# A channel mixer whose down projection multiplies paired halves of 512 columns, with the eight sample tokens served by gathered rows

## The chip, the cores and the metric

The kernel runs on one core of a Trainium2 chip. The metric is device time in microseconds (us) of one execution. TensorE is PE in the profile (its weight loads are PEld), VectorE is DVE, ScalarE is ACT, GpSimd is POOL, and SyncE, which issues the DMAs, is SP.

## What is computed

One inference step of a trunk of two layers with width 1024, for 256 prompt tokens and 8 sample tokens (264 together, `T`). Each layer has a recurrent mixer and then the channel mixer `peer_ffn`, on which the change works. Per token, eight heads choose 16 of 16384 experts each; an expert is one row `u[e]` of the up table and one row `v[e]` of the down table:

```python
e = i1 * PEER_KEYS + i2
gate = jax.nn.softmax(top_s, axis=-1)
act = jax.nn.gelu(jnp.einsum('thed,td->the', u[e], xb).astype(F32), approximate=False)
return jnp.einsum('the,thed->td', (gate * act).astype(xb.dtype), v[e])
```

## The kernel before

The kernel doesn't gather rows. For all 264 tokens it computes all 16384 products with `u`, applies Gelu, multiplies by a gate that is zero for every expert not chosen, and multiplies the result by all of `v`. Both tables are cut into 128 tiles of 128x1024 float32 (512 KB each). In each of the two channel mixers the order on TensorE is: 16 query tiles (with the scores of the heads between them), 128 up tiles, 128 down tiles. The first mixer's up and down tiles run from about 460 us to 1270 us of the span, the second's from about 1700 us to 2494 us.

**Split operands.** Every float32 operand is split into an upper part (rounded to float32r) and a lower part (the rest), and a product is the sum of three: upper by upper, upper by lower, lower by upper. So each tile takes 8 x 3 = 24 matmuls, in `Ring.products` (L378) for query and up tiles and in `Ring.product` (L362 to L364) for down tiles, where each of eight PSUM banks `sums[d]` collects over all 128 tiles.

**The ring of weights.** `Ring` has three slots. SP loads a tile into `weights_raw` (`load_to`, L337) when the lower half of the tile three back has been made; ACT casts it to the upper half (`make_hi`, L347) when TensorE has finished the tile three back; POOL subtracts to make the lower half (`make_lo`, L355). All three run through the same list of tiles in order.

**Up tiles.** ACT applies Gelu to each product (L779, L781). The gates of four tokens at a time (a quad, 66 in all) are built on DVE (`build`, L836 to L841), multiplied out to 128 columns per token by 12 bf16 matmuls (L705), copied by ACT (L786) and applied by DVE (`apply`, L856; `gate_tile`, L848). There is one quad per up tile from tile 38 on.

**Down tiles.** For each, ACT makes the upper half of the gated activations (`make_gated_hi`, L742) and DVE the lower half (`make_gated_lo`, L860), in a ring of three. At the end DVE adds the eight sums to the residual `x` (L884), ACT squares it (L205), and TensorE sums the squares by a matmul with ones (L231), from which the next norm starts. A stage of the program is a block, and at its end all engines wait for each other.

**Samples.** The 8 sample tokens are columns 256 to 263 of every product. Their gates are brought into the layout of the prompt's by two matmuls, two copies and five transposes around up tiles 34 to 36.

## Time and profile before

| | us |
|---|---|
| three runs | 2503.45, 2504.04, 2508.36 |
| median | 2504.04 |
| span of the profiled execution | 2507.1 |

Which of the three runs was profiled isn't recorded; its span of 2507.1 us lies 1.3 us below the highest run and 3.1 us above the median. In the rows below, PE busy is the time in which at least one matmul was in flight, and since matmuls overlap, a busy PE says less than the number of matmuls per microsecond (the number behind the x). PEclk is the clock that TensorE was granted, as a share of the full 2.4 GHz. "Idle before" is the idle time of an engine just before an instruction, with what released it. POOL is busy for 67% of the span, DVE for 68%.

### The profile page before, as it was taken

What the parts mean: (1) busy time and instruction counts of PE and PEld (TensorE: products, weight loads), DVE (VectorE), ACT (ScalarE), POOL (GpSimd) and SP (SyncE); (2) the same over time, 40 slices, a digit from 0 to 9 for tenths busy, and PEclk for the clock granted to TensorE, in tenths of its full rate; (3) what the DMA queues carried; (4) which work ended last, traced back from release to release, by engine and by line L of the source; (5) the groups of instructions that cost most, each with busy time, mean ns of one, the idle gap of its engine ahead of it and who ended that gap; (6) DMA issues with size and microseconds to landing.
All of it is one profiled execution on the core that took longest, in us unless ns stands there. A gap on an engine that the chain in (4) does not pass through costs nothing. (4 is left out here: it accounts for less than half of the span.)

```text
span 2507.1 us, 46304 instructions
## 1 busy us (share of the span) xinstructions
PE 2330.1 (93%) x19024; PEld 2217.5 (88%) x19024; DVE 1713.6 (68%) x2773; ACT 1112.0 (44%) x1893; POOL 1669.8 (67%) x716
## 2 busy tenths in 40 slices
PE   6977978999999999999979875899999999999998
PEld 5957858999999999999979722899999999999998
DVE  4776553795678268888868376349767762888887
ACT  4512234455554444444446412344555444444443
POOL 4714016687666788888867544758766668888885
PEclk9978988999999999999989977899999999999999
DMA  4410013454444555555535443445544445555553
GB/s 156 153 52 34 35 44 135 144 185 160 144 144 144 169 184 178 184 178 184 179 123 169 157 151 109 133 137 163 176 146 147 145 147 182 180 182 181 181 182 131
DMA packets 102226, 370.27 MB, mean 148 GB/s; under 512 B 15392, under 2 KB 15744, under 8 KB 98816
## 3 DMA queue, kind: packets, MB, share of 16 engines
q1 hardware_dynamic: 102016, 367.30, 45.4%
q8 instruction: 152, 2.49, 0.4%
q14 instruction: 58, 0.48, 0.1%
HBM read 352.67 MB, written 14.58 MB: 146 GB/s over the span
## 5 line engine op out<-in xcount | busy, mean ns | idle before, releaser
L355 POOL TENSOR_TENSOR weights_halves<-weights_raw,weights_halves 128x1024 fp32r<-128x1024 f32 x638 | 1541.6, 2419 | 571.1 <-ACT weights_halves L347 570.8
L347 ACT CAST weights_halves<-weights_raw 128x1024 fp32r<-128x1024 f32 x638 | 669.9, 1051 | 936.2 <-PE peer L378 482.6
L860 DVE TENSOR_TENSOR gated<-acts,gated 128x264 fp32r<-128x264 f32 x256 | 615.3, 2405 | 127.5 <-ACT gated L742 127.5
L378 PE MATMUL peer<-ffn_in_hi,weights_halves 128*128 128x264 f32 x4608 | 650.7, 288 | 14.9 <-ACT ffn_in_hi L271 14.9
L378 PEld LDWEIGHTS peer<-ffn_in_hi,weights_halves 128*128 128x128 f32 x4608 | 590.9, 189 | 22.0 <-issue 16.6
L364 PE MATMUL peer<-gated,weights_halves 128*128 128x264 f32 x2048 | 583.2, 285 | 0.0
L362 PE MATMUL peer<-gated,weights_halves 128*128 128x264 f32 x2048 | 581.2, 284 | 0.0
L363 PE MATMUL peer<-gated,weights_halves 128*128 128x264 f32 x2048 | 579.9, 283 | 0.0
L363 PEld LDWEIGHTS peer<-gated,weights_halves 128*128 128x128 f32 x2048 | 385.9, 188 | 0.0
L362 PEld LDWEIGHTS peer<-gated,weights_halves 128*128 128x128 f32 x2048 | 385.4, 188 | 0.0
L364 PEld LDWEIGHTS peer<-gated,weights_halves 128*128 128x128 f32 x2048 | 384.4, 188 | 0.0
L378 PE MATMUL peer<-ffn_in_lo,weights_halves 128*128 128x264 f32 x2304 | 326.9, 285 | 0.0
L378 PEld LDWEIGHTS peer<-ffn_in_lo,weights_halves 128*128 128x128 f32 x2304 | 298.4, 189 | 0.0
L848 DVE TENSOR_TENSOR acts<-peer,acts 128x264 f32<-128x264 f32 (+44 forms) x178 | 59.2, 333 | 200.2 <-ACT peer L781 200.0
L378 PE MATMUL projected<-mix_in_hi,weights_halves 128*128 128x264 f32 x1120 | 158.9, 291 | 26.6 <-ACT mix_in_hi L271 21.2
L378 PEld LDWEIGHTS projected<-mix_in_hi,weights_halves 128*128 128x128 f32 x1120 | 145.3, 191 | 33.1 <-issue 18.3
L841 DVE TENSOR_TENSOR gated_room<-gated_room,peer 128x768 bf16<-128x768 bf16 x264 | 133.6, 548 | 0.0
L856 DVE TENSOR_TENSOR acts<-peer,acts 128x156 f32<-128x156 f32 (+21 forms) x132 | 99.1, 751 | 41.8 <-ACT acts L786 40.1
L705 PE MATMUL peer<-gated_room 128*128 128x128 bf16 x1584 | 113.9, 219 | 0.0
L742 ACT CAST gated<-acts 128x264 fp32r<-128x264 f32 x256 | 104.0, 408 | 0.0
L705 PEld LDWEIGHTS peer<-gated_room 128*128 128x128 bf16 x1584 | 91.0, 97 | 7.1
L786 ACT COPY acts<-peer 128x356 f32<-128x356 f32 (+21 forms) x132 | 81.4, 617 | 0.0
(465 smaller groups left out, 2359.3 us busy)
## 6 DMA issues: line engine op xcount, KB each, us to landing
weights_raw<-in_up SPq DMA_DIRECT2D x256, 512.0 KB, 3.5
weights_raw<-in_down SPq DMA_DIRECT2D x256, 512.0 KB, 3.5
weights_raw<-in_ssm_w_in SPq DMA_DIRECT2D x40, 512.0 KB, 3.4
weights_raw<-in_w_q SPq DMA_DIRECT2D x32, 512.0 KB, 3.4
weights_raw<-in_ab_w_in SPq DMA_DIRECT2D x30, 512.0 KB, 3.5
weights_raw<-in_ssm_w_out SPq DMA_DIRECT2D x16, 512.0 KB, 3.5
states<-in_ssm_in SPq DMA_DIRECT2D x8, 1024.0 KB, 7.4
ssm_sample<-states SPq DMA_DIRECT2D x8, 1024.0 KB, 4.8
```

Source lines behind the costliest of these rows:

```text
L347: act.copy(self.halves[:, 0, slot, :], self.raw[:, slot, :]).then_inc(self.hi_made, 1)
L355: pool.tensor_tensor(self.halves[:, 1, slot, :], self.raw[:, slot, :], self.halves[:, 0, slot, :].bitcast(F32), ALU.subtract).then_inc(sel ...
L362: pe.matmul(out, hi, rhs_hi, start=start, stop=False, skip_group_check=True)
L363: pe.matmul(out, hi, rhs_lo, start=False, stop=False, skip_group_check=True)
L364: return pe.matmul(out, lo, rhs_hi, start=False, stop=stop, skip_group_check=True)
L378: ins = pe.matmul(out, self.halves[:, half, n % RING, at], both[side], start=start and half == 0 and side == 0 and k == 0, stop=stop and h ...
L705: last = pe.matmul(gate_banks[quad % 2][:, t * KEYS:(t + 1) * KEYS], one_hot[:, quad % 2, t // 2, :, t % 2], weighted[:, quad % 2, part, t ...
L742: core.gated_hi.inc(act.copy(a_hi[:, j % RING, :], acts[:, j, :]))
L786: core.gates_stored.inc(act.copy(acts[:, j + 1:KEYS, 4 * quad:4 * quad + 4].rearrange("p k t -> p t k"), gate_banks[quad % 2][:, :].rearra ...
L841: last = dve.tensor_tensor(weighted[:, quad % 2, :, a], equal[:, a].unsqueeze(1).broadcast_to(shape), gates_t[:, :, pair].unsqueeze(2).bro ...
L856: core.gates_applied.inc(dve.tensor_tensor(to, got, to, ALU.mult))
L860: core.gated_lo.inc(dve.tensor_tensor(a_lo[:, j % RING, :], acts[:, j, :], a_hi[:, j % RING, :].bitcast(F32), ALU.subtract))
```

## The change

The prompt's 256 tokens and the 8 samples go separate ways in the up and down stages.

- **Down tiles.** The gated activations lie as pairs, upper and lower half side by side (`a_pairs`, 512 columns). One matmul of 512 columns multiplies the upper weights by both halves, and one of 256 columns adds lower weights by upper activations into the second half of the bank (`pair_product`). A tile has 8 x 2 = 16 matmuls in place of 24. `FIRST_PAIRED = KEYS` leaves the up tiles unpaired, so `pair_products`, `add_halves` and the copies into `cross` are in the source and run nowhere.
- **Up tiles.** They keep three matmuls, of 256 columns in place of 264, from the buffer `pairs`, which two DMAs on SP's queue fill from the norm's output. Query tiles keep 264 columns.
- **Lower weights.** For down tiles they are made on DVE (`make_lo_on_dve`) in place of POOL.
- **Gates.** 64 quads in place of 66, spread over up tiles 40 to 122.
- **Samples.** The samples' inputs are spread to 128 rows (8 tokens x 16 choices) by eight float32 matmuls after the first query tile. In the down stage POOL gathers, head by head, the 128 chosen rows of `u` and then of `v` by indirect DMA (16 of 512 KB per stage); DVE takes the dot products (`dot`) and the weighted sum (`weigh`), every sixth tile; eight small float32 matmuls in the last down tile add up the 16 rows of a token.
- **End of the stage.** DVE adds each bank to `x` in two steps, one for each half.

```diff
+FIRST_PAIRED = KEYS
+QUAD_TILES = 84
+GATED_AHEAD = 124
+FIRST_DOT = 10
+FIRST_WEIGHTED = 64
+SAMPLE_STEP = 6
+SAMPLES_AFTER = 3
...
+    def pair_product(self, pe, out, n, cols, pair, start, stop):
 
         hi, lo = self.halves[:, 0, n % RING, cols], self.halves[:, 1, n % RING, cols]
-        pe.matmul(out, hi, rhs_hi, start=start, stop=False, skip_group_check=True)
-        pe.matmul(out, hi, rhs_lo, start=False, stop=False, skip_group_check=True)
-        return pe.matmul(out, lo, rhs_hi, start=False, stop=stop, skip_group_check=True)
-
+        pe.matmul(out, hi, pair, start=start, stop=False, skip_group_check=True)
+        return pe.matmul(out[:, SEQ:2 * SEQ], lo, pair[:, 0:SEQ], start=False, stop=stop, skip_group_check=True)
...
+    def make_lo_on_dve(self, dve, n):
+
+        slot = n % RING
+        dve.wait_ge(self.hi_made, n + 1)
+        dve.tensor_tensor(self.halves[:, 1, slot, :], self.raw[:, slot, :],
+                          self.halves[:, 0, slot, :].bitcast(F32), ALU.subtract).then_inc(self.lo_made_dve, 1)
...
             @block.sync
             def _(sp):
                 ring.load_to(sp, first + RING + 1)
                 core.load(sp, keys, sub_keys)
+                sp.wait_ge(core.norm_hi.sem, norm.hi0 + KC)
+                halves_paired.inc(sp.dma_start(pairs[:, :, 0:SEQ].bitcast(F32),
+                                                    h_hi[:, :, 0:SEQ].bitcast(F32)), 16)
+                sp.wait_ge(core.norm_lo_pool.sem, norm.pool0 + KC // 2)
+                sp.wait_ge(core.norm_lo_dve.sem, norm.dve0 + KC // 2)
+                halves_paired.inc(sp.dma_start(pairs[:, :, SEQ:2 * SEQ].bitcast(F32),
+                                                    h_lo[:, :, 0:SEQ].bitcast(F32)), 16)
                 ring.load_to(sp, end + RING)
...
+                ring.make_lo(pool, down)
+                pool.wait_ge(core.sample_copied.sem, kinds0 + 1)
+                pool.wait_ge(ring.multiplied, down)
+                for n in range(2 * PEER_HEADS):
+                    if n >= GATHER_SLOTS:
+                        pool.wait_ge(gather_used.sem, used0 + n - GATHER_SLOTS + 1)
+                    head = n % PEER_HEADS
+                    gathered[n % GATHER_SLOTS].inc(pool.indirect_dma_start(
+                        out=slots[:, n % GATHER_SLOTS, :], out_offset=None, in_=(up_rows, down_rows)[n // PEER_HEADS],
+                        in_offset=bass.IndirectOffsetOnAxis(ap=expert[:, head:head + 1], axis=0)), 16)
                 ring.make_lo(pool, end + RING)
...
                 for j in range(KEYS):
                     tile = down + j
-                    pe.wait_ge(ring.lo_made, tile + 1)
+                    pair = a_pairs[:, j % RING, :]
+                    ring.await_lo(pe, tile)
...
+                        if j == KEYS - 1 and d == SAMPLES_AFTER:
+                            pe.wait_ge(cross_added.sem, crossed0 + 4)
+                            pe.wait_ge(gather_used.sem, used0 + 2 * PEER_HEADS)
+                            for k in range(KC):
+                                summed = pe.matmul(sums[1][:, k * DEC:(k + 1) * DEC], weighted_sum[:, columns[k]],
+                                                   core.row_token, start=True, stop=True)
+                            sample_ready.inc(summed)
...
-                for j in range(RING, KEYS):
-                    make_gated_lo(j)
+                    if j >= KEYS - RING:
+                        ring.make_lo_on_dve(dve, down + j - (KEYS - RING))
+                for j in range(KEYS):
+                    if j + RING < KEYS:
+                        ring.make_lo_on_dve(dve, down + j + RING)
+                        make_gated_lo(j + RING)
```

Three places of the program show how the order moves. First, DVE from the last up tiles into the down stage of the first mixer. Before (`gated` is the ring of gated activations, `peer_n` a PSUM bank):

```order
L848 TENSOR_TENSOR acts<-peer_2,acts 128x264
L848 TENSOR_TENSOR acts<-peer_0,acts 128x264
L848 TENSOR_TENSOR acts<-peer_1,acts 128x264
L848 TENSOR_TENSOR acts<-peer_2,acts 128x264
L860 TENSOR_TENSOR gated_3588<-acts,gated_3588 128x264 x125
L884 TENSOR_TENSOR x<-peer_3,x 128x264
```

In this place DVE has one subtraction per down tile. The same place after the change, on DVE (L967 is `gate_tile`, L391 `make_lo_on_dve`, L983 `make_gated_lo`):

```order
L967 TENSOR_TENSOR acts<-peer_0,acts 128x256
L391 TENSOR_TENSOR weights_halves_110<-weights_raw,weights_halves_110 128x1024
L967 TENSOR_TENSOR acts<-peer_1,acts 128x256
L391 TENSOR_TENSOR weights_halves_110<-weights_raw,weights_halves_110 128x1024
L967 TENSOR_TENSOR acts<-peer_2,acts 128x256
L391 TENSOR_TENSOR weights_halves_110<-weights_raw,weights_halves_110 128x1024 x2
L983 TENSOR_TENSOR gated_3606<-acts,gated_3606 128x256
L391 TENSOR_TENSOR weights_halves_110<-weights_raw,weights_halves_110 128x1024
L983 TENSOR_TENSOR gated_3606<-acts,gated_3606 128x256
```

A subtraction over a whole weight tile now stands ahead of each of the activations'. Second, SP at the start of the first channel mixer, after the change (`ffn_pairs` is `pairs`):

```order
L363 DMA weights_raw<-in_w_q 128x1024
L134 DMA acts<-in_sub_keys 128x2048
L701 DMA ffn_pairs_3605<-query_in_hi_3607 128x8x256
L705 DMA ffn_pairs_3605<-query_in_lo_3608 128x8x256
L363 DMA weights_raw<-in_w_q 128x1024 x12
```

The two new transfers, each behind a wait for the norm, stand ahead of the loads of the query tiles from the fifth on. Third, TensorE in the last down tile, after the change (L401 and L402 are `pair_product`, L831 the samples' sum, L247 the squares):

```order
L401 MATMUL peer_6<-gated_3606,weights_halves_110 128x512
L402 MATMUL peer_6<-gated_3606,weights_halves_110 128x256
L831 MATMUL peer_4<-row_token,ffn_pairs_room 128x8 x8
L401 MATMUL peer_7<-gated_3606,weights_halves_110 128x512
L402 MATMUL peer_7<-gated_3606,weights_halves_110 128x256
L401 MATMUL peer_0<-gated_3606,weights_halves_110 128x512
L402 MATMUL peer_0<-gated_3606,weights_halves_110 128x256
L401 MATMUL peer_1<-gated_3606,weights_halves_110 128x512
L402 MATMUL peer_1<-gated_3606,weights_halves_110 128x256
L401 MATMUL peer_2<-gated_3606,weights_halves_110 128x512
L402 MATMUL peer_2<-gated_3606,weights_halves_110 128x256
L247 MATMUL peer_3<-acts,ones 128x264 x8
```

The samples' matmuls stand after the fourth of the eight banks, and the other four banks wait behind them.

## Rows read from the trace of the kernel before

**Rows 1.** The page: busy time, share of the span and instructions of each engine.

```profile
PE 2330.1 (93%) x19024; PEld 2217.5 (88%) x19024; DVE 1713.6 (68%) x2773; ACT 1112.0 (44%) x1893; POOL 1669.8 (67%) x716
```

**Rows 2.** Busy time by stretches: up with quads, down, query and up.

```profile
core 0: us, PE busy (x) PEld busy (x) DVE busy (x) ACT busy (x) POOL busy (x), PEclk, DMA share, GB/s
704.00:804.00 100.00, 100.00 (x989) 98.50 (x988) 78.13 (x165) 50.01 (x109) 65.56 (x28) 1.00 0.46 143
...
1000.00:1250.00 250.00, 250.00 (x2060) 250.00 (x2059) 207.56 (x86) 117.15 (x172) 205.66 (x87) 1.00 0.58 182
...
1700.00:1780.00 80.00, 80.00 (x663) 80.00 (x663) 76.59 (x235) 41.07 (x63) 66.75 (x28) 1.00 0.55 172
```

**Rows 3.** Groups of instructions by line: count, busy time, mean ns, idle before.

```profile
L355 POOL TENSOR_TENSOR weights_halves<-weights_raw,weights_halves 128x1024 fp32r<-128x1024 f32 x638 | 1541.6, 2419 | 571.1 <-ACT weights_halves L347 570.8
L347 ACT CAST weights_halves<-weights_raw 128x1024 fp32r<-128x1024 f32 x638 | 669.9, 1051 | 936.2 <-PE peer L378 482.6 <-PE peer L364 391.6 <-PE projected L378 20.9
L860 DVE TENSOR_TENSOR gated<-acts,gated 128x264 fp32r<-128x264 f32 x256 | 615.3, 2405 | 127.5 <-ACT gated L742 127.5
L742 ACT CAST gated<-acts 128x264 fp32r<-128x264 f32 x256 | 104.0, 408 | 0.0
L547 DVE TENSOR_TENSOR acts<-peer,acts 128x4096 f32<-128x4096 f32 x4 | 17.7, 4426 | 0.1
```

**Rows 4.** The instructions of one line each: ns min/median/max, first and last start.

```profile
L860 DVE TENSOR_TENSOR gated<-acts,gated x256: 419/2418/2627, 877.3 to 2486.6; 128x264 fp32r<-128x264 f32 x128
...
L259 DVE TENSOR_TENSOR ffn_in_lo<-acts,ffn_in_hi x8: 420/420/422, 408.1 to 1633.6; 128x264 fp32r<-128x264 f32 x8
...
L1389 PEld LDWEIGHTS reads<-p,w_room x64: 186/192/333, 239.3 to 273.1; 128*128 128x128 f32 x64
...
L2339 PE MATMUL scan<-states,c_mask x64: 592/617/1062, 1448.5 to 1541.5; 128*32 128x512 f32 x64
```

**Rows 5.** Timeline of plain float32 work: start, us, count.

```profile
243.78 0.97 PEld L1381 LDWEIGHTS spread<-ident,p 128*128 128x128 f32 x8
244.68 0.97 PEld L1389 LDWEIGHTS reads<-p,w_room 128*128 128x128 f32 x8
...
1458.72 1.04 PE L2339 MATMUL scan<-states,c_mask 128*32 128x512 f32 x2
```

**Rows 6.** The first stretch of rows 2, the gates' matmuls of L705 alone.

```profile
704.00:804.00 100.00, 23.98 (x336) 19.30 (x336) 1.00 0.46 143
```

**Rows 7.** Who waited for whom: us in total, times, longest us.

```profile
DVE gated_room L836 <- PE peer L693: 23.3, 2, 11.6
```

**Rows 8.** DMA issues: number, KB each, median us from issue to landing.

```profile
weights_raw<-in_down SPq DMA_DIRECT2D x256, 512.0 KB, 3.5
...
acts<-in_sub_keys SPq DMA_DIRECT2D x2, 1024.0 KB, 5.7
...
ssm_prompt<-state SPq DMA_DIRECT2D x1, 1024.0 KB, 3.9
```

**Rows 9.** Timeline at the start of the first channel mixer.

```profile
400.50 0.43 SPq L125 DMA_DIRECT2D acts<-in_sub_keys  x1
400.98 47.94 SPq L337 DMA_DIRECT2D weights_raw<-in_w_q  x12
...
408.14 1.45 DVE L259 TENSOR_TENSOR ffn_in_lo<-acts,ffn_in_hi 128x264 fp32r<-128x264 f32 x4
...
412.90 1.05 ACT L347 CAST weights_halves<-weights_raw 128x1024 fp32r<-128x1024 f32 x1 [4.24 <-PE peer L378]
```

**Rows 10.** Timeline at the end of the second channel mixer.

```profile
2491.38 2.96 DVE L884 TENSOR_TENSOR x<-peer,x 128x264 f32<-128x264 f32 x8 [2.36 <-PE peer L364]
...
2491.85 2.95 ACT L205 ACTIVATE acts<-x 128x264 f32<-128x264 f32 x8 [5.27 <-DVE x L884]
...
2493.71 3.72 PE L231 MATMUL peer<-acts,ones 128*128 128x264 f32 x16
```

More of the change, by code:

```diff
@@ L21 @@
 SSM_SLOTS = 3
+GATHER_SLOTS = 3
 class Count:
@@ L86, in __init__ @@
         self.ids_turned = Count(nc, "ids_turned")
+        self.gathered = [Count(nc, f"gathered{i}") for i in range(GATHER_SLOTS)]
         self.gates_built = Count(nc, "gates_built")
@@ L442 @@
 KINDS = 5
-QUADS = T // 4
-EXP_TILE = 22
-TURN_TILE = 36
-FIRST_GATED = 38
-GATED_AHEAD = 120
+QUADS = SEQ // 4
+EXP_TILE = 24
+TURN_TILE = 38
+FIRST_GATED = 40
+FIRST_PAIRED = KEYS
[5 more added lines that the diff above has]
+SAMPLES_AFTER = 3
+GELU_TILE = FIRST_DOT + SAMPLE_STEP * PEER_HEADS
+QUAD_AT = {FIRST_GATED + q * QUAD_TILES // QUADS: q for q in range(QUADS)}
 class Room:
@@ L651, in score @@
                     core.head_scored.inc(last)
-                def tile_product(tile, out):
-                    ring.products(pe, out, tile, [(h_hi[:, k, :], h_lo[:, k, :]) for k in range(KC)],
-                                  [slice(k * P, (k + 1) * P) for k in range(KC)], start=True,
-                                  stop=True, norm=norm if tile == first else None).then_inc(ring.multiplied, 1)
+                columns = [slice(k * P, (k + 1) * P) for k in range(KC)]
                 for s in range(SETS):
@@ L660, in _ @@
                         pe.wait_ge(core.query_copied.sem, copied0 + s - RING + 1)
-                    tile_product(first + s, projected[s % RING][:, 0:T])
+                    ring.products(pe, projected[s % RING][:, 0:T], first + s,
+                                  [(h_hi[:, k, :], h_lo[:, k, :]) for k in range(KC)], columns, start=True, stop=True,
+                                  norm=None if s else norm).then_inc(ring.multiplied, 1)
+                    if s == 0:
+                        pe.wait_ge(rows_copied.sem, rows_copied0 + 1)
+                        for k in range(KC):
+                            last = pe.matmul(row_banks[k // 4][:, (k % 4) * P:(k % 4 + 1) * P],
+                                             sample_rows[:, k * P:(k + 1) * P], core.ident, start=True, stop=True)
+                        rows_spread.inc(last)
+                    if s == 5:
+                        pe.wait_ge(rows_copied.sem, rows_copied0 + 2)
                     if s >= 3 and s % 2:
@@ L672, in _ @@
                         pe.wait_ge(core.tile_gated.sem, gated0 + j - RING - FIRST_GATED)
-                    tile_product(up + j, projected[bank][:, 0:T])
+                    if j == 0:
+                        pe.wait_ge(halves_paired.sem, paired0 + 32)
+                    if j < FIRST_PAIRED:
+                        last = ring.products(pe, projected[bank][:, 0:SEQ], up + j,
+                                             [(pairs[:, k, 0:SEQ], pairs[:, k, SEQ:2 * SEQ]) for k in range(KC)],
+                                             columns, start=True, stop=True)
+                    else:
+                        last = ring.pair_products(pe, projected[bank][:, :], up + j,
+                                                  [pairs[:, k, :] for k in range(KC)], columns)
+                    last.then_inc(ring.multiplied, 1)
                     if j == 0:
@@ L782, in _ @@
                     core.gelu_made.inc(last)
-                    quad = j - FIRST_GATED
-                    if 0 <= quad < QUADS:
+                    quad = QUAD_AT.get(j)
+                    if quad is not None:
                         act.wait_ge(core.gates_made.sem, gates0 + quad + 1)
@@ L2847, in program @@
             sources += [d[name][n] for n in tiles]
-        core.ring = Ring(core, ctx, sources)
+        on_dve = {first[name] + j for name in ("down0", "down1") for j in range(KEYS)}
+        core.ring = Ring(core, ctx, sources, on_dve)
         with nc.Block() as block:
```

222 lines of the change are left out of this document (161 added, 61 removed).

## The prediction

> **What bounds the kernel now.** I read the page first: PE is busy for 93% of the span, no other engine for more than 68% [rows 1]. Then the stretches. In the down stage, in the up stage and among the quads TensorE has no idle time, at the full clock [rows 2], so there the time is the number of matmuls by the interval between them. In the down stage that is 250 us / 2060 = 121.4 ns, in the up stage 80 / 663 = 120.7 ns, where 264 columns at 2.4 GHz are 110.0 ns; so a float32r matmul has 10.7 to 11.4 ns beyond its columns. The others wait for TensorE: ACT's casts were idle for 936 us, nearly all of it behind its matmuls [rows 3]. DVE's subtraction of 128x264 takes 2405 ns in the mean [rows 3], but 420 ns at its shortest and in another place [rows 4]: it is long only beside POOL's subtraction, which takes 2419 ns [rows 3].
>
> **The change, part by part.** All terms are made against the profiled execution, whose span of 2507.1 us is 3.1 us above the median of 2504.04; I carry the difference over to the median.
>
> *Down tiles.* Per bank three matmuls of 264 columns, 3 x 121.4 = 364.2 ns, become one of 512 and one of 256. No float32r matmul of either width is in the trace. The bounds for 256: no gain, 121.4 ns, and the weight load alone. That load is seen where eight of them stand behind matmuls of one column: (0.97 - 0.19) / 7 = 111 ns [rows 5], 0.19 us being the length of one [rows 4]. For 512: plain float32 matmuls of 512 columns follow each other at 1.04 - 0.62 = 0.42 to 0.43 us [rows 4, 5], twice what their columns take, so 215 ns for one pass; and above, the present interval scaled by columns, 121.4 x 512 / 264 = 235.4 ns. I take the value nearest to the rows of the same form, columns / 2.4 GHz plus the present excess of 11.4 ns: 213.3 + 11.4 = 224.7 and 106.7 + 11.4 = 118.1, in sum 342.8. That saves 21.4 ns per bank, and with 8 banks, 128 tiles and 2 stages (2048) **43.8 us**. The bounds are 11 ns (22 us) and 38 ns (78 us).
>
> *Up tiles.* 6144 matmuls lose 8 columns: 3.33 ns each, **20.5 us**; bounds nothing, and 120.7 - 111 = 9.7 ns, 60 us.
>
> The Trainium skill (TensorE: Matmul & The Clock Gate, Back-to-back issue gap) gives columns / 2.4 GHz plus 2.5 ns for an isolated matmul. For 264 columns that is 112.5 ns, and the rows of the same width show 121, so here it doesn't hold as it stands. Used for differences alone it would make the down stage's saving 12.5 ns per bank, 25.6 us, and the sum 2467 us.
>
> *Gates.* Among the quads, 989 matmuls in 100 us, 336 of them the gates' [rows 2, 6]: (100 - 653 x 0.1207) / 336 = 63 ns each. Two quads fewer are 24 matmuls per stage: **3.0 us** for both. Spreading the quads moves DVE's work to later tiles and costs TensorE nothing: with one quad per 3.6 us DVE was busy for 78% [rows 2]. The last up tiles gain work (three lower activations at tile 124, three weight tiles after 125 to 127), about 1.2 us per 2.8 us tile. Turning the gates waits two tiles longer; DVE had waited 11.6 us for it [rows 7], so nobody is late.
>
> *Lower weights on DVE.* DVE takes 4426 ns for 4096 elements [rows 3], so 1.1 to 1.2 us for 1024, and 0.42 us for the activations, once POOL is silent: 1.6 us per tile. A down tile lasts 8 x 0.3428 = 2.74 us. ACT has 1.05 + 0.41 us per tile [rows 3]. From the release of a slot the upper half takes 1.1 us, the lower 1.2 us, and TensorE wants it two tiles (5.5 us) later; the slot's load then has 3.5 us [rows 8] and is wanted three tiles after the release. Every sixth tile DVE has a dot product or a weighted row more, 1.2 us: 2.8 us, within that slack. Nothing on the path; the cover is 1.1 us of DVE per tile, and if it goes each us over costs 256 us in all.
>
> *The pairs' DMAs.* SP waits for the norm's last lower part (408.14 + 1.45 [rows 9]), then the two transfers of 1 MB and only then the loads of the fifth and later query tiles, which now are issued at 400.98 [rows 9]. One of 1 MB takes 3.9 to 5.7 us [rows 8]; the first can go at 409, so both have landed by 419 and the load behind them by 420 to 422. The first query tile ends at 412.9 [rows 9], tiles take 2.9 us, and ACT needs the fifth at 420.5 plus the row matmuls' 1.8 us. The stall is 0 to 3 us per stage; I take 1, **2 us** in all.
>
> *Spreading the samples' rows.* Eight plain float32 matmuls of 128 columns are sixteen records in the trace (as L231's eight are [rows 10]) at (0.97 - 0.19) / 7 = 111 ns [rows 5]: 1.8 us per stage, on the path, **3.6 us**. ACT's copy ahead of them (1.05 us) falls into its idle 4.24 us [rows 9].
>
> *End of the stage.* Now, counted from the end of the first bank: TensorE ends 7 x 0.364 = 2.5 us later, and the squares' sum takes 3.7 us [rows 10], in all 6.3. DVE follows at 0.37 us per bank (2.96 / 8 [rows 10]). After: DVE has two dependent additions per bank, about 0.85 us. TensorE stands after the fourth bank (1.0 us) until DVE has the first two (1.9), has sixteen records at 111 ns (3.8), and ends its banks at 5.2. DVE has four banks at 3.6, waits for the samples until 4.0, adds them in 0.6, and ends at 4.6 + 4 x 0.85 = 8.0; a square and the last of the sums make 9.1. So 2.8 us more per stage, **5.6 us**; were the additions no slower than now, it would be about 1 us.
>
> *Constants.* One more block and reduction at the start: **1 us** taken, 0 to 2.
>
> The gathers are hidden: 16 transfers of 512 KB per stage, two tiles' worth of time apart or more, at a DMA share of 0.58 [rows 2]; the first is wanted ten tiles into the stage.
>
> Sum: -43.8 - 20.5 - 3.0 + 2 + 3.6 + 5.6 + 1 = **-55 us**: 2452 us for the profiled execution, **2449 us** for the median.
>
> **The rivals.** The costs other than the matmuls' and gates' sum to +12.2, the gates save 3.0, as above.
>
> *The excess goes with the columns* (the moving operand's reads are slow): 512 takes 235.4 and 256 117.7, saving 11.1 x 2048 = 22.7 us below and 3.7 x 6144 = 22.5 above: -36, 2468 us. For it: at full clock the excess is there in every float32r row. Against: plain float32 of 512 columns has only 2 ns beyond its columns per pass [rows 5].
>
> *The weight load is the limit.* An interval of 121 is then set by a load of 111 ns and its handing over, not by columns: 256 columns stay at 121.4 and 120.7, and 512 hide the load, 215. Down saves 27.8 x 2048 = 56.9 us, up nothing: -48, 2456 us. For it: load and columns differ by 1 ns only [rows 5].
>
> *The excess is the 264's own* (a width beyond 256): 256 at 111 and 512 at 215 save 38.2 x 2048 = 78 and 9.7 x 6144 = 60 us: -129, 2375 us. For it: matmuls whose two passes over 128 columns stream as long as 256 would are spaced at 111 ns [rows 5]. Against: they read half as much.
>
> *Slower: DVE becomes the bound of the down stage.* If the 1024-wide subtraction takes DVE what it takes POOL, 2.42 us, a tile needs 2.42 + 0.42 = 2.84 us and a hand-over, as much as now; the down stage gains nothing, and 32 dot products and weighted rows of 2.42 us come on top. -20.5 - 3.0 + 12.2 + 77 = +66, 2570 us. It decides once DVE's work passes 2.74 us per tile. For it: in this stage every one of its subtractions is long [rows 4]. Against: 420 ns for the same form when POOL is silent. The Trainium skill (SBUF — State Buffer, Who interferes with whom) says that DVE with two SBUF inputs and a reading GpSimd exclude each other for whole instructions; the trace agrees, 420 beside 2418 ns.
>
> *The gathers come late.* No row shows a DMA that POOL issues, nor one by indices. DVE waits for them in its queue, and the lower weights stand behind. A slot is filled again within 18 tiles, 49 us; 512 KB take 3.5 us [rows 8]. Beyond that point each us is one us for 26 gathers; 2.1 us over would undo the gain, 2504 us. That would also be the case in which the samples' separate way doesn't do what it says, to take work off TensorE's path.
>
> **How the numbers follow.** Forecast 0.40, columns 0.20, weight load 0.15, the 264's own 0.13, DVE 0.04, late gathers 0.08 (half of it the same, half slower). Within 0.2%, 5 us, a measurement of this kernel can't tell a difference. So faster 0.88, same 0.04, slower 0.08. The range takes in the first three cases and the bounds of the small terms, and reaches towards the fourth: 2405 to 2482 us.
>
> **What would show it.** In the profile after: no idle PE in the up and down stages; down tiles every 2.74 us (16 matmuls; 2.69 if the load limits, 2.82 if columns do); up tiles every 24 x 0.1174 = 2.82 us; DVE's 128x1024 subtraction near 1.2 us and the activations' near 0.42; SP's two pairs within 10 us of the norm and no gap before the fifth query tile; PE idle below 1 us after the fourth bank of the last tile. Down tiles above 2.9 us, or DVE waits for gathers, would make the prediction wrong.

## The result and the profile after

The changed kernel takes 2476.52 us (median of four runs, 2475.88 to 2477.74), the kernel before beside it 2506.2 us: ratio 0.9883, 95% interval 0.9869 to 0.9897. It is 29.7 us faster, where 55 were forecast; 2449 was the predicted time, and 2476.5 lies in its range, near the slow end. The profiled executions differ by 33.0 us of span (2507.1 and 2474.1). The page of the changed kernel, its first part [rows 1]:

```profile
span 2474.1 us, 42397 instructions
## 1 busy us (share of the span) xinstructions
PE 2297.1 (93%) x16988; PEld 2094.7 (85%) x16988; DVE 1555.0 (63%) x3085; ACT 1097.1 (44%) x1927; POOL 1109.8 (45%) x492
```

TensorE is still what bounds it. The stretches: two are the same as in [rows 2] (up with quads; query and up), the other two are the middle of either down stage:

```profile
core 0: us, PE busy (x) PEld busy (x) DVE busy (x) ACT busy (x) POOL busy (x), PEclk, DMA share, GB/s
704.00:804.00 100.00, 100.00 (x964) 99.05 (x962) 67.10 (x141) 48.93 (x109) 69.99 (x30) 1.00 0.46 153
...
1700.00:1780.00 80.00, 80.00 (x669) 80.00 (x668) 78.49 (x181) 39.85 (x60) 69.73 (x29) 1.00 0.54 182
```

```profile
950.00:1200.00 250.00, 250.00 (x1430) 217.88 (x1429) 155.30 (x200) 121.08 (x180) 19.39 (x11) 1.00 0.61 211
2150.00:2400.00 250.00, 250.00 (x1430) 218.18 (x1429) 154.91 (x200) 121.40 (x180) 21.23 (x12) 1.00 0.63 213
```

There is no idle PE in either stage, as before. A bank (one of the eight PSUM banks of a down tile) takes two matmuls. In the down stage 1430 matmuls in 250 us are 2 x 250 / 1430 = 0.3497 us per bank, and a tile comes every 2.80 us: 2.74 was forecast, 2.82 if the excess went with the columns. In the up stage the interval, from the start of one matmul to the start of the next, is 80 / 669 = 119.6 ns; it was 120.7. The groups that answer to [rows 3]:

```profile
L384 POOL TENSOR_TENSOR weights_halves<-weights_raw,weights_halves 128x1024 fp32r<-128x1024 f32 x382 | 928.2, 2435 | 530.4 <-ACT weights_halves L373 530.0
L391 DVE TENSOR_TENSOR weights_halves<-weights_raw,weights_halves 128x1024 fp32r<-128x1024 f32 x256 | 313.7, 1225 | 272.6 <-ACT weights_halves L373 270.5
L720 POOL DMA_INDIRECT ffn_pairs_room<-in_up_rows,expert x16 | 26.9, 1679 | 191.3 <-DVE expert_act L991 178.3
L983 DVE TENSOR_TENSOR gated<-acts,gated 128x256 fp32r<-128x256 f32 x256 | 110.0, 431 | 0.0
```

DVE's subtraction of 1024 elements takes 1.225 us, that of the activations 431 ns, as forecast (1.2 and 0.42): with POOL silent the rows of 2405 ns are gone. DVE waits for ACT, not for gathers, and POOL for DVE.

From the first and last starts of TensorE's matmuls in each stage, the 33.0 us come apart as follows (both mixers together, after less before):

- down tiles, first to last start, 127 of them: 370.27 to 355.64 us, twice: -29.3 (14.4 ns per bank; with the 128th tile -29.5)
- up stages: the projections' matmuls -8.3 (1.35 ns each), the gates' -2.7, the rest -1.0
- query stages with the spread rows: +1.84 and +1.56 = +3.4
- last tile and squares' sum, up to the start of the sum's last matmul: 6.23 us before in both mixers, 10.57 and 8.91 after: +7.0
- the mixer between, whose code is the same: -2.1; before the first query and after the last sum -0.1

The end of the first channel mixer in the timeline (start, length in us):

```profile
1248.82 0.42 DVE L1044 TENSOR_TENSOR x<-peer,x 128x256 f32<-128x256 f32 x1
1249.16 0.41 DVE L1043 TENSOR_TENSOR x<-peer,x 128x256 f32<-128x256 f32 x1
1249.30 1.95 PE L831 MATMUL peer<-row_token,ffn_pairs_room 128*128 128x8 f32 x16 [0.71 <-DVE x L1044]
...
1251.29 0.41 DVE L1050 TENSOR_TENSOR x<-peer,x 128x8 f32<-128x8 f32 x4 [0.47 <-PE peer L831]
...
1252.80 5.18 PE L247 MATMUL peer<-acts,ones 128*128 128x264 f32 x16
...
1254.57 0.42 DVE L1044 TENSOR_TENSOR x<-peer,x 128x256 f32<-128x256 f32 x1
```

TensorE stands 0.71 us for DVE and then has 1.95 us of sample sums, 2.7 in all, as the forecast had it. But the squares' sum takes 5.18 us here, and 3.72 in the second mixer, the same 3.72 as before [rows 10]. The granted clock tells why:

```profile
1249.00:1252.00 3.00, 2.70 (x21) 2.61 (x22) 2.42 (x10) 0.51 (x2) 1.76 (x1) 1.00 0.00 0
1252.30:1255.70 3.40, 3.40 (x10) 2.65 (x10) 2.59 (x7) 2.39 (x7) 0.00 (x0) 0.51 0.00 0
1256.00:1258.00 2.00, 1.98 (x9) 1.34 (x8) 0.00 (x0) 0.38 (x1) 1.54 (x1) 1.00 0.00 0
```

After the idle 0.71 us and the matmuls of eight columns the clock is 0.51 of full for 3.4 us, the lower level of 1.2 GHz, and then full again. In the second mixer it stays full at this place. The fall is the rule and not an accident of one profile: the changed kernel and experiments 1 to 4, 7, 8 and 11 have the same samples' sum in the last tile, and of the sixteen ends in their profiles thirteen show it. Such a place in experiment 8, in the second mixer:

```profile
2460.30:2463.60 3.30, 3.30 (x9) 2.57 (x8) 2.39 (x7) 1.93 (x6) 0.00 (x0) 0.50 0.00 0
```

Those thirteen ends take 10.5 to 10.6 us from the start of the last tile to the start of the sum's last matmul, the other three 8.9. In the twelve ends of the kernel before and of experiments 5, 6, 9, 10 and 12, whose end is another, the clock stays full.

### The profile page after: what moved, and what is told of

Same layout as the page of the kernel before. It is cut to its first block and busy times, and to the rows that moved or that the text cites. A ratio compares the mean times of both kernels' runs of the same rounds, so it can differ in the third digit from the quotient of the medians.

```text
span 2474.1 us, 42397 instructions
## 1 busy us (share of the span) xinstructions
PE 2297.1 (93%) x16988; PEld 2094.7 (85%) x16988; DVE 1555.0 (63%) x3085; ACT 1097.1 (44%) x1927; POOL 1109.8 (45%) x492
## 5 line engine op out<-in xcount | busy, mean ns | idle before, releaser
L384 POOL TENSOR_TENSOR weights_halves<-weights_raw,weights_halves 128x1024 fp32r<-128x1024 f32 x382 | 928.2, 2435 | 530.4 <-ACT weights_halves L373 530.0
L426 PE MATMUL peer<-ffn_pairs,weights_halves 128*128 128x256 f32 x6144 | 769.1, 285 | 0.0
L426 PEld LDWEIGHTS peer<-ffn_pairs,weights_halves 128*128 128x128 f32 x6144 | 744.4, 191 | 0.7 <-issue 0.7
L401 PE MATMUL peer<-gated,weights_halves 128*128 128x512 f32 x2048 | 717.4, 393 | 0.0
L402 PE MATMUL peer<-gated,weights_halves 128*128 128x256 f32 x2048 | 571.6, 279 | 0.0
L391 DVE TENSOR_TENSOR weights_halves<-weights_raw,weights_halves 128x1024 fp32r<-128x1024 f32 x256 | 313.7, 1225 | 272.6 <-ACT weights_halves L373 270.5
L401 PEld LDWEIGHTS peer<-gated,weights_halves 128*128 128x128 f32 x2048 | 383.7, 187 | 91.4
L402 PEld LDWEIGHTS peer<-gated,weights_halves 128*128 128x128 f32 x2048 | 383.8, 187 | 0.0
L967 DVE TENSOR_TENSOR acts<-peer,acts 128x4 f32<-128x4 f32 (+28 forms) x174 | 52.1, 299 | 184.0 <-ACT peer L897 184.0
L720 POOL DMA_INDIRECT ffn_pairs_room<-in_down,expert x16 | 27.6, 1723 | 274.8 <-DVE ffn_pairs_room L1004 122.3
L979 DVE TENSOR_TENSOR acts<-peer,acts 128x164 f32<-128x164 f32 (+42 forms) x128 | 119.0, 930 | 31.6 <-ACT acts L902 29.9
L720 POOL DMA_INDIRECT ffn_pairs_room<-in_up_rows,expert x16 | 26.9, 1679 | 191.3 <-DVE expert_act L991 178.3
L983 DVE TENSOR_TENSOR gated<-acts,gated 128x256 fp32r<-128x256 f32 x256 | 110.0, 431 | 0.0
L852 ACT CAST gated<-acts 128x256 fp32r<-128x256 f32 x256 | 102.4, 402 | 0.0
L426 PEld LDWEIGHTS peer<-query_in_hi,weights_halves 128*128 128x128 f32 x512 | 69.1, 196 | 20.7 <-issue 15.3
```

The source lines that it names most:

```text
L384: pool.tensor_tensor(self.halves[:, 1, slot, :], self.raw[:, slot, :], self.halves[:, 0, slot, :].bitcast(F32), ALU.subtract).then_inc(sel ...
L391: dve.tensor_tensor(self.halves[:, 1, slot, :], self.raw[:, slot, :], self.halves[:, 0, slot, :].bitcast(F32), ALU.subtract).then_inc(self ...
L401: pe.matmul(out, hi, pair, start=start, stop=False, skip_group_check=True)
L402: return pe.matmul(out[:, SEQ:2 * SEQ], lo, pair[:, 0:SEQ], start=False, stop=stop, skip_group_check=True)
L426: ins = pe.matmul(out, self.halves[:, half, n % RING, at], both[side], start=start and half == 0 and side == 0 and k == 0, stop=stop and h ...
L720: gathered[n % GATHER_SLOTS].inc(pool.indirect_dma_start(out=slots[:, n % GATHER_SLOTS, :], out_offset=None, in_=(up_rows, down_rows)[n // ...
```

## The experiments

There are twelve kernels, each timed beside the kernel before. The theories at the start were about two numbers: the two matmuls of a bank cost 350 ns where 343 were forecast, and in the up stage a float32r matmul of 256 columns costs 120 where 117 were.

### 1. Widths on an idle chip

The changed kernel with a block after its end in which TensorE alone has series of 48 matmuls:

```diff
+                for n in range(48):
+                    pe.matmul(banks[n % 8][:, 0:512], w(n), hi[:, 0:512], start=True, stop=True)
```

> The changed kernel with a block appended in which TensorE works alone: series of 48 matmuls of one width each, weights of 128x128 changing every time. Theory A (the moving stream of float32r takes about 0.455 ns per column, and under it a new weight tile can't be taken more often than every 120 ns): 128, 192 and 256 columns at 120 ns, 264 at 121, 320 at 146, 384 at 175, 512 at 233; 512 and 256 in turn 233 and 118. Theory B (the prediction's: columns at 2.4 GHz plus a fixed 11.4 ns): 128 at 111 or less, 256 at 118, 264 at 121, 320 at 145, 384 at 171, 512 at 225. Theory C (the weight load is the only limit): 121 up to 264 columns, then columns alone, 133, 160, 213. Weights of 64 columns under 256 moving columns: A and C expect them below 120 if the load is shorter for them, B 118 all the same. bfloat16 has no such excess in any theory: 128 at 58, 256 at 107 to 112, 512 at 213 to 218. Time: 3 to 5 % of the block's own on top, some 120 us over the changed kernel.

Measured, mean ns from start to start at full clock:

| columns | 128 | 192 | 256 | 264 | 320 | 384 | 512 |
|---|---|---|---|---|---|---|---|
| float32r | 110.6 | 112.3 | 120.3 | 120.1 | 146.6 | 173.4 | 227.5 |
| bfloat16 (all ones) | 56.1 | | 109.1 | 112.5 | | | 215.8 |

In turn 512 and 256 took 236.5 + 116.3. 256 columns with weights of 64 columns took 113 (the median; one interval of 306 lifts the mean to 118), and 256 columns read from 8 columns further 118. Two of the rows (ns min/median/max of one, first and last start):

```profile
L3085 PE MATMUL probe<-weights_halves x48: 280/281/287, 2507.5 to 2513.1; 128*128 128x264 f32 x48
L3091 PE MATMUL probe<-weights_halves x48: 387/389/397, 2528.6 to 2539.3; 128*128 128x512 f32 x48
```

(2513.1 - 2507.5) / 47 = 119 and (2539.3 - 2528.6) / 47 = 228 ns. None of the three theories holds over all widths. 264 to 256 columns saves nothing here, and 512 has 14 ns beyond its columns. Theory A's floor of 120 falls with 128 and 192 columns at 111 and 112, and its 0.455 ns per column with 512. Theory C falls with 320 and up. B names every measured width within 3 ns, with 13 to 14 ns in place of 11.4 from 320 columns on; but its rule would give 91 for 192 columns, where 112 was measured, and 3.3 ns between 256 and 264, where there are none. The bfloat16 series are columns / 2.4 plus 2.4 to 2.8 ns. The Trainium skill (TensorE: Matmul & The Clock Gate, Back-to-back issue gap) gives columns / 2.4 plus 2.5 for an isolated matmul, and these rows, in which each matmul has its own weight load, agree with that (56.1 and 215.8 ns). The same section's figures for a stream of loads and matmuls, about 81 ns at 128 columns and 131 at 512, they don't show. It is float32r that has 8 to 12 ns more from 256 columns on.

### 2. Three matmuls of 256 in the down stage

```diff
-        pe.matmul(out, hi, pair, start=start, stop=False, skip_group_check=True)
+        pe.matmul(out[:, 0:SEQ], hi, pair[:, 0:SEQ], start=start, stop=False, skip_group_check=True)
+        pe.matmul(out[:, SEQ:2 * SEQ], hi, pair[:, SEQ:2 * SEQ], start=False, stop=False, skip_group_check=True)
```

> Down stage as three matmuls of 256 columns per bank, all else as changed (2476.5). Theory A (a floor of 120 ns per float32r matmul, 512 columns at 233): 360 - 350.2 = 9.8 ns per bank, 2048 banks, +20 us: 2496. Columns alone (0.455 ns each, no floor): 353 - 350.2, +6: 2482. The prediction's fixed excess: 354.3 - 342.8, +24 against its own down stage. Weight load alone at 121.4: +29: 2505.

2497.22 us, ratio 0.9963 (0.9949 to 0.9977). The down stage:

```profile
950.00:1200.00 250.00, 250.00 (x2085) 250.00 (x2084) 150.12 (x195) 117.82 (x175) 20.15 (x11) 1.00 0.63 206
```

250 / 2085 = 119.9 ns, 360 per bank: the size that A named, +20.7 us against the changed kernel. So the pairing is worth 21 us, and all the other parts together 9 us.

### 3. Lower weights back on POOL

The calls of `make_lo_on_dve` for the down tiles go, and POOL makes them between its gathers.

```diff
-        on_dve = {first[name] + j for name in ("down0", "down1") for j in range(KEYS)}
+        on_dve = set()
```

> The lower weights of the down stage go back to POOL, the gathers between them; the pairs of 512 columns stay. Theory H (hidden: whichever engine makes them, TensorE's matmuls set the tile of 2.80 us): POOL's and DVE's subtractions are 2.4 us each beside one another, both below 2.80, and the time stays within 5 us of 2476.5. Rival D (DVE is the bound then): in six tiles it has six subtractions of 2.4 us and a dot product or weighted row of 2.4 us or more, 16.8 of 16.8 us, and POOL six of 2.4 us and a gather's issue of 1.7: tiles rise to 2.9 us and the time by 10 to 30 us, 2487 to 2507.

2531.89 us, ratio 1.0102 (1.0085 to 1.0119): slower than the kernel before, and 25 us beyond the slowest that rival D named. The tiles last 2.80 us except around the samples' steps, where most often one lasts 4.2 to 5.0; the excess over 2.80 is 28.5 us in the first stage and 26.4 in the second. Such a place, DVE, ACT and POOL in the timeline, and then who waited for whom in that down stage:

```profile
1112.12 2.42 DVE L987 TENSOR_TENSOR gated<-acts,gated 128x256 fp32r<-128x256 f32 x1 [0.38 <-ACT gated L856]
1114.47 1.27 DVE L1008 SCALAR_TENSOR_TENSOR ffn_pairs_room<-ffn_pairs_room,expert_act 128x1024 f32<-128x1024 f32 x1
1114.48 0.40 ACT L856 CAST gated<-acts 128x256 fp32r<-128x256 f32 x1
1114.66 5.88 POOL L384 TENSOR_TENSOR weights_halves<-weights_raw,weights_halves 128x1024 fp32r<-128x1024 f32 x2 [0.40 <-ACT weights_halves L373]
1115.66 2.61 DVE L987 TENSOR_TENSOR gated<-acts,gated 128x256 fp32r<-128x256 f32 x1
```

```profile
ACT weights_halves L373 <- DMA weights_raw<-in_down: 30.2, 16, 3.3
PEld peer L401 <- POOL weights_halves L384: 27.5, 16, 2.3
PE peer L401 <- DVE gated L987: 22.5, 14, 2.0
```

The weighted row takes 1.27 us where DVE had 0.38 to spare, and POOL's two subtractions beside it 5.88 us in place of 4.8. POOL is late, the slot comes free late, the load and ACT's cast behind it are late, and TensorE waits.

The row alone doesn't do it. POOL's next instruction at that place is the issue of a gather, and the long tile, of 4.72 us, starts 4 us behind it. At 1189 us the same row has no gather behind it:

```profile
1120.68 0.97 POOL L724 DMA_INDIRECT ffn_pairs_room<-in_down,expert  x1
...
1189.23 1.27 DVE L1008 SCALAR_TENSOR_TENSOR ffn_pairs_room<-ffn_pairs_room,expert_act 128x1024 f32<-128x1024 f32 x1
1189.43 10.96 POOL L384 TENSOR_TENSOR weights_halves<-weights_raw,weights_halves 128x1024 fp32r<-128x1024 f32 x4 [0.40 <-ACT weights_halves L373]
```

There POOL falls behind as well (10.96 us in place of 9.6), catches up within its own spare time, and no tile is longer; so it is with the last three rows of either stage. Of the 13 gathers that follow a row in a stage, 12 have a tile of 4.5 to 4.9 us that starts within 4 us of them. So the trace lays the loss on row and gather together; no run took out one of the two.

### 4. Up tiles paired as well

```diff
-FIRST_PAIRED = KEYS
+FIRST_PAIRED = 40
```

> The up tiles from the 40th on are paired as well (88 tiles per stage): one matmul of 512 and one of 256 columns per bank, the cross half copied by ACT and added by DVE. If TensorE stays the bound: 360 - 350.2 = 9.8 ns x 8 x 88 x 2 = 13.8 us less, 2463. Rival: the copy and the addition lie between a tile's last matmul and its gating, DVE has 78 % of a tile's time among the quads already, and the banks come free too late; each tile then waits: a wait of 0.08 us per paired tile undoes it, 0.3 us makes 2515.

2464.99 us, ratio 0.9831 (0.9814 to 0.9847). The up stages are 6.4 us shorter each (6.9 forecast), the time 11.5. In the first up stage TensorE waited for DVE 0.2 us in all, so the rival's waits didn't come.

### 5 and 6. No samples, and no samples with POOL

The fifth leaves out the samples' separate way, so the eight sample columns of x get nothing from the channel mixers: no spread rows (`L754`), gathers (`L720`), dot products, weighted rows (`dot`, `weigh`) or sum (`L831`). The sixth leaves out the same, and has the edit of the third.

```diff
                 for j in range(KEYS):
...
                         make_gated_lo(j + RING)
-                    if j >= FIRST_DOT and (j - FIRST_DOT) % SAMPLE_STEP == 0 and (j - FIRST_DOT) // SAMPLE_STEP < PEER_HEADS:
-                        dot((j - FIRST_DOT) // SAMPLE_STEP)
...
```

> The samples' separate way through the channel mixer left out (no rows spread, no gathers, dot products, weighted rows or sum; the eight sample columns get no addition from the mixer). By the prediction's terms it cost TensorE 1.8 us per stage for the spread rows and part of the end of the stage: in the changed kernel's end TensorE stood 0.7 us and had 1.95 us of sample matmuls, but the end is DVE's sixteen additions at 0.79 us per bank, which stay, so only 0.5 to 1 us per stage goes. All else is hidden: 2 x (1.8 + 0.7) = 5 us less than 2476.5, 2471.5. Rival (dot products, weighted rows and gathers slow the down tiles): more than 10 us less, below 2466. Rival (the samples' sum is the end): 2 x (1.8 + 2.7) = 9 less, 2467.5.

> As the previous kernel (the samples' way left out), and the lower weights of the down stage made by POOL. With the samples' work in it this move cost 55 us (2531.9), in tiles of 4.5 to 4.7 us, one for each dot product or weighted row. Theory S (only the samples' work on DVE doesn't fit beside subtractions that last 2.4 us each; without it all fits into 2.80 us): the same as the previous kernel within 5 us, about 2472. Rival P (subtractions of 2.42 us on two engines don't fit even so, or the ring's loads come late): 2490 or more.

2469.57 us (0.9848, 0.9832 to 0.9865) and 2470.20 us (0.9849, 0.9833 to 0.9866): seven less than with the samples, and no difference between DVE and POOL. The stages give the same seven: the query stages are 1.6 and 1.7 us shorter without the spread rows, the ends 2.8 and 1.1, 1.7 of it the clock, and the down tiles come in the same 2.80 us. The sixth kernel's groups in the middle of the down stage:

```profile
L950 DVE TENSOR_TENSOR gated<-acts,gated 128x256 fp32r<-128x256 f32 x90 | 218.3, 2426 | 33.7 <-ACT gated L828 33.7
L384 POOL TENSOR_TENSOR weights_halves<-weights_raw,weights_halves 128x1024 fp32r<-128x1024 f32 x90 | 216.4, 2405 | 35.6 <-ACT weights_halves L373 35.6
```

Both subtractions last 2.4 us beside each other, both fit into a tile of 2.80 with 0.37 us to spare, and PE isn't idle. So the move to DVE gains nothing by itself; it is what makes room for the samples' work. That work costs 7 us with the move and 62 without it (2531.9 - 2470.2). Theory S, which laid this on DVE's share alone, isn't shown so far: here POOL's gathers are gone too. In the fifth kernel the last tile and the sum take 7.79 us in both mixers, between 6.23 and 8.91. There the matmuls of the sum start 327 ns apart in place of 222: DVE's two additions per bank are the end, 1.6 us more than one each.

### 7. Eight of 512, then eight of 256

```diff
-                        last = ring.pair_product(pe, sums[d][:, :], tile, columns[d], pair, start=j == 0,
-                                                 stop=j == KEYS - 1)
+                        if j < KEYS - 1:
+                            pe.matmul(sums[d][:, :], ring.halves[:, 0, tile % RING, columns[d]], pair, start=j == 0,
+                                      stop=False, skip_group_check=True)
...
```

> In the down stage eight matmuls of 512 columns and then eight of 256 per tile, instead of one of each in turn (the last tile in turn). The matmul of 512 measured 227.5 ns among its like with all other engines idle and 232.3 in the kernel. Theory O (the change of width costs 5 ns): 2048 x 5 = 10 us less, 2466. Theory N (the width of the neighbour doesn't matter; it is the operands' addresses, or the other engines' traffic): 2476.5 within 3 us.

2484.42 us, ratio 0.9906 (0.9889 to 0.9923): 8 us slower, so neither theory. 1416 matmuls in 250 us are 353 ns per bank; tiles take 2.827 us. In the mean a matmul of 512 took 234 ns (232 in turn) and one of 256 120 (118 in turn).

### 8 and 11. What the excess hangs on

More blocks after the end of the changed kernel, built like the first; that of 11 has the transfers beside its second half:

```diff
+                    pe.matmul(banks[n % 8][:, 0:512], w(n), hi[:, 520:1032], start=True, stop=True)
...
+                    count.inc(sp.dma_start(ring.raw[:, n % RING, :], ring.sources[n]), 16)
```

> The changed kernel with two blocks appended. First TensorE alone: 224, 240, 248, 272, 288 columns; 264 columns with 64-wide weights, and with the same weights every time; 512 with the same weights, with moving operands that change, with 24 weight tiles, into one bank; eight of 512 and eight of 256 in groups; 512 and 256 in turn into one bank as in the down stage. Then 256, 264, 512 and 512/256 in turn while DVE subtracts and ACT copies 1024 elements in SBUF without pause. If a weight load of 111 ns is a floor and the columns have 13.4 ns of their own beyond 2.4 GHz (320 to 512 measured so): 224 at 112, 240 at 114 to 120, 248 at 117 to 120, 272 at 127, 288 at 133, 264 with 64-wide weights at 116 to 120. If the excess is the load's (a load next to a stream that just outlasts it): 264 with unchanged weights at 120 still, since it is loaded anyway. 512 at 227 in all forms if neither addresses nor weights matter; in turn 350. Beside DVE and ACT: the same within 1 ns if SBUF traffic doesn't matter, 5 ns more per 512 columns if it is what the kernel's 232 come from.

> What makes the matmul of 512 columns 232 ns in the kernel and 227 among its like: TensorE alone with 512 and 256 columns that accumulate into eight banks (start and stop only at the ends), with the two in turn and the second one's moving operand elsewhere, with 512 columns read from 8 columns further, with 448 and 480 columns; then 256, 512, 256, and 512/256 in turn while 30 transfers of 512 KB come in. Theory K (accumulating into PSUM costs it): 232 accumulating, 227 writing. Theory L (DMA traffic costs it): 227 alone, 232 beside the transfers. Theory M (the change of width alone): 227 in both, 236 in turn. 448 at 200 and 480 at 213 if the excess of 13.4 ns stays the same from 320 columns up.

Mean ns: 224 and 240 columns 112, 248 115, 272 125.4, 288 131.8, 448 202.6, 480 216.7. 264 columns with weights of 64 columns 120, with the same weights every time 120. 512 columns 227 with unchanged weights, with 24 weight tiles, with moving operands that change, into one bank, and accumulating. 512 and 256 in turn 236 + 117; in groups of eight 229 and 119. 512 with the moving operand 8 columns (32 bytes) further 233. Beside DVE and ACT without pause, the windows of 264 and of 512 columns, and then 512 beside the transfers:

```profile
2614.00:2624.50 10.50, 10.50 (x90) 10.50 (x89) 10.19 (x10) 10.18 (x11) 0.00 (x0) 1.00 0.01 2
2626.00:2646.00 20.00, 20.00 (x90) 16.55 (x89) 19.45 (x17) 19.40 (x20) 0.00 (x0) 1.00 0.00 1
```

```profile
2575.00:2595.00 20.00, 20.00 (x90) 16.55 (x89) 0.00 (x0) 0.00 (x0) 0.00 (x0) 1.00 0.92 322
```

DVE and ACT are busy for 97% and the DMA engines for 92%, and the intervals stay at 120 and 227 ns, as alone. So neither the SBUF traffic of DVE and ACT nor transfers (theory L) nor accumulating (K) costs these matmuls anything. Nor does the weight load set the 120 of 264 columns, since half the weights' columns leave it; at 256 columns they bring 113, so there the load has a share. Up to 240 columns all take 111 to 112, the interval of the load [rows 5]. What is left is the width, the neighbour's width (M) and the place where the moving operand starts.

### 9 and 10. The right halves added early

In the ninth the last down tile puts its three products into the left halves, so that DVE adds the right ones a tile earlier. The tenth has `FIRST_PAIRED = 40` too.

```diff
+                        if j == KEYS - 1:
+                            pe.wait_ge(cross_added.sem, crossed0 + d + 1)
+                            last = ring.last_product(pe, sums[d][:, 0:SEQ], tile, columns[d], pair)
```

> The changed kernel with another end of the channel mixer: the last down tile puts all three products into the left half of each bank (three matmuls of 256), so that DVE adds the right halves to x while TensorE is at the last two tiles, and the samples' sum stands in a right half after the second bank. After the last matmul one addition per bank is left (0.37 us) and not two (0.79). TensorE has 8 x 10 ns more, no idle 0.71 us. From the start of the last tile the additions now end at 8.1 us; then at 6 x 0.36 + 0.72 + 1.95 + 0.4 = 5.3, about 2.8 us earlier per stage: 5.5 us less, 2471. Rival (the end is set by ACT's squares or by the sum of squares, which then take over): 2 us less, 2474.5 or nothing.

> The end of the previous kernel and the paired up tiles from the 40th on (2465.0 by themselves). The two don't touch each other: 2465.0 - 5.5 = 2459.5. Rival (half or more of it lost to something shared): 2463 or more.

The ninth: 2475.77 us, ratio 0.9869 (0.9854 to 0.9884), which the measurement can't tell from 0.9883. From the first down matmul to the last of the squares' sum it takes 363.6 us in both mixers, where the changed kernel took 366.2 and 364.5: 2.6 and 0.9 less, and the 2.6 has the 1.7 us of clock in it. The mixer between took 4.7 us more in this profile (358.9), which hides it in the span. Its timeline at the same place:

```profile
1250.94 2.74 DVE L1065 TENSOR_TENSOR x<-peer,x 128x256 f32<-128x256 f32 x8
1251.40 2.74 ACT L221 ACTIVATE acts<-x 128x264 f32<-128x264 f32 x8 [2.09 <-DVE x L1065]
1252.66 3.72 PE L247 MATMUL peer<-acts,ones 128*128 128x264 f32 x16
```

DVE is done before the sum is half through: the sum's own 3.72 us behind TensorE's last bank are the end, and the additions had been beside them. So the rival of this expectation named the right end. Its size, 2 us or nothing, holds for an end at full clock; against the 10.5 to 10.6 us that thirteen of sixteen ends take, the 8.0 of both ends here are 2.5 to 2.6 less each, most of it clock that is kept. TensorE doesn't stand before the samples' sum here, and which of the two, the idle time or the order of the work, keeps the clock full no run tells apart.

The tenth: 2459.73 us, ratio 0.9809 (0.9795 to 0.9822), and its interval lies clear of the changed kernel's: 16.8 us less than that. It is 5.3 less than the fourth, as forecast (5.5), but not by shorter additions: the fourth's ends take 10.5 us each, both with the lower clock, and the tenth's 8.0.

### 12. The moving operand 32 bytes further

The tenth kernel with this edit, and in its second mixer also with the groups of the seventh.

```diff
-        a_pairs = a_ring[:, 0:RING * 2 * SEQ].rearrange("p (r t) -> p r t", r=RING)
+        a_pairs = a_ring[:, 8:8 + RING * 2 * SEQ].rearrange("p (r t) -> p r t", r=RING)
```

> The faster kernel (the early right halves and the paired up tiles, 2459.7) with the down stage's moving operands 32 bytes further on in every partition; in the second channel mixer also eight matmuls of 512 and then eight of 256 per tile. With all other engines idle 512 columns took 227 ns from one start and 233 from 32 bytes further, 8 of 512 and 8 of 256 in groups took 348 per pair from the first start, and in turn 352.8; in the kernel, whose operands start like the second, in turn 350.2 and in groups 353.4 (tiles of 2.800 and 2.827 us). Theory U (the start of the moving operand sets it, as in the idle series): first mixer 352.8 x 8 = 2.82 us per tile, second 2.78; in sum -2.6 + 2.5 = no change, 2460. Theory V (the start costs 5 ns wherever it is off): both at 227 + 118: tiles of 2.76, 10 us less, 2450. Theory W (the start matters only in a series of one width): 2.80 and 2.827, 3 us more, 2463.

2460.76 us, ratio 0.9820 (0.9803 to 0.9836), as the tenth. Tiles take 2.81 us in the first mixer, in turn (2.80 in the tenth), and 2.799 and 2.821 by turns in the second, in groups. None of the three theories met both. The start changes the pattern of the intervals of 512 columns (234, 233, 225 by turns, in place of 233, 231) and hardly the mean: 230.7 + 120.6 per bank in place of 232.3 + 117.9.

## Why the prediction was right in sign and too large

- **Down tiles** (forecast -43.8, measured -29.5). This is the step that failed: "columns / 2.4 GHz plus the present excess of 11.4 ns" for 512 columns, 224.7 ns. The trace has 232.3 for 512 and 117.9 for 256 columns, in sum 350.2. The 118.1 for 256 in the pair was right; 512 has 19 ns beyond its columns, 14 of which an idle chip shows too. The mechanism held, the size was two thirds. The plain float32 rows, 2 ns beyond the columns per pass [rows 5], were no measure for float32r. The lower bound of 11 ns per bank isn't the sum of its own two bounds either: 364.2 - 235.4 - 121.4 leaves 7.4 ns, 15 us. The measured 14.4 ns lies above both.
- **Up tiles** (-20.5, measured -8.3). The same step: the excess was taken as fixed, while 256 and 264 columns take the same 120 ns alone, and 1.35 ns less here. That is close to the lower bound (nothing) that the text kept.
- **Gates** -3.0, measured -2.7. **Rows and pairs' DMAs** +3.6 and +2, measured +3.4 for both. Experiment 5, without the rows, has the query stages of the kernel before within 0.3 us, so the rows cost all of it and the transfers next to nothing. **Constants** +1, measured 0.
- **End of the stage** +5.6, measured +5.4 plus 1.7 of clock. The size came out by luck: the forecast had DVE's additions as the end (9.1), but TensorE's own 0.71 + 1.95 us made the 2.7 per stage, with the squares' sum behind them. The forecast's own working has that path too, at 5.2 + 3.7 = 8.9, and passed over it for being 0.2 shorter. Experiment 9 shows it: with one addition per bank in place of two the end at full clock went from 8.9 to 8.0, of which 0.7 is the idle time that is gone. That is still 1.8 us per stage over the kernel before, so "about 1 us" for quicker additions left TensorE's path out too. The fall of the clock was in no term.
- **Lower weights on DVE** 0, and 0 it was. That POOL could not have kept them was not weighed: experiment 3 puts 55 us on it, more than the change gains. The gathers were hidden, as forecast: in experiment 5, without them, the down tiles come no faster.

Of the rivals, "the excess goes with the columns" came nearest in time (-36, against -33.0 in the profile) and in the down pair (235.4 + 117.7). In the time that was luck, since two misses cancel in part: it had -22.7 for the down tiles where -29.5 was measured, and -22.5 for the up tiles where it was -8.3. Experiment 1 refutes its rule: from 320 to 512 columns the interval grows by 0.42 ns per column, 1 / 2.4 GHz. "The 264's own" is refuted by the equal intervals of 256 and 264, "the weight load" by 264 columns at the same 120 with weights half as wide, and by 227 where it wanted 215. "DVE becomes the bound" didn't come, but its mechanism, subtractions of 2.4 us on two engines at once, is what left 0.4 us per tile in experiment 3, too little for rows and gathers.

The model that the runs leave for float32r at full clock, with weights of 128 columns, is a table and no formula: 111 to 112 ns up to 240 columns, 120 at 256 and 264, columns / 2.4 plus 12 to 17 ns from 272 on. Where widths change or the operand starts elsewhere, a 512 takes 4 to 9 ns more and a 256 up to 4 less. Why the excess has this size, and why it moves with neighbour and start, stays open.

## What to carry to other kernels

Price a matmul by a row of its own width and type; where there is none, keep the range open on both sides and put a series of 48 such matmuls behind a kernel, which costs one run. Where a change has parts, ask of each what happens to the others without it: the move that gained nothing alone carried the rest. And at the end of a stage look for what follows on the busy engine before counting another engine's additions as the path, and at the granted clock there before reading a gain of 2 us out of it.

## What the hardware showed beyond expectation

- float32r matmuls of 256 and of 264 columns both take 120 ns alone, and 248 take 115 (experiments 1 and 8): shortening 264 to 256 saved 1.35 ns each in the kernel.
- TensorE's mean intervals didn't move by 1 ns beside DVE and ACT at 97% (experiment 8) and beside DMA engines at 92 to 99% (experiment 11).
- After about 0.7 us idle and 1.95 us of matmuls of eight columns the granted clock fell to its lower level for 3.4 us in thirteen of sixteen ends, and stayed full in the other three after the same work; it cost up to 1.7 us each time.
- The mixer between, the same code in every kernel here, took from 351.6 to 358.9 us from one profile to the next. In it the granted clock was at its lower level for 88 to 104 us, and mostly longer where the mixer took longer (102 at 358.9, 90 at 351.6), which goes with the difference but doesn't account for it. A sum over stages told more than the spans.
